# The first weight unit behind five norms takes x times the gain, and the root factor and the shift come to its result

## The chip, the cores and the metric

The kernel runs on one core of one Trainium2 chip. Its time is the device time of one execution in microseconds (us); for the kernel before there are three runs. Engines: TensorE (PE) does the matrix products, VectorE (DVE) and ScalarE (ACT) work elementwise, GpSimd (POOL) issues one stream of DMAs, SyncE (SP) another. Each engine takes its own instructions in program order, and engines wait for each other on semaphores.

## The reference

Two blocks follow one another on one sequence of 512 tokens with 1024 features. The first has six residual branches, each behind a norm whose result is scaled and shifted by a condition. Cut to what matters here:

```
rms_norm(x, g)   = x * rsqrt(mean(x*x) + eps) * g
modulate(h)      = h * (1 + scale) + shift

norm 0: x += 0.5 * gate * swiglu(h)        norm 3: x += 0.5 * gate * swiglu(h)
norm 1: x += gate * pool_mixer(h)          norm 4: x += gate * conv_mixer(h)
norm 2: x += 0.5 * gate * swiglu(h)        norm 5: x += 0.5 * gate * swiglu(h)

swiglu(h)        = (silu(h @ w_a) * (h @ w_b)) @ w_out        (1024 -> 2816 -> 1024)
conv_mixer(h)    = (b * causal_conv3(c * v)) @ w_out,  b, c, v = h @ w_in
```

After a final norm the second block takes x through norm 6, attention and a gated linear attention whose branches are merged and projected back, and then through norm 7:

```
x = x + gate2 * (square(relu(modulate(rms_norm(x, norm2)) @ w_mlp1)) @ w_mlp2)      (1024 -> 4096 -> 1024)
```

All is f32. The scale and the gain are per feature, the root factor is per token.

## The kernel before

**Layout.** Features lie on the partitions: x is `X`, eight tiles (k = 0 to 7) of 128 features by 512 tokens. A product's stationary operand is a 128x128 piece of a weight, its moving operand a 128x512 tile of the activations.

**Products.** Each f32 product is made of three in a 32-bit format that keeps fewer bits: weight high x h high (L1684), weight high x h low (L1685), weight low x h high (L1686). Weights are cut into numbered units of 128x2048 (a pair of result tiles over all eight k, 16 x 3 = 48 products; the output projections of an FFN have units of 128x1408, one result tile, 33 products). SyncE loads a unit into one of two slots of `W_RAW`; ScalarE casts it to `W_HI` (`split_hi`, L584); VectorE subtracts to get `W_LO` (`split_lo`, L979); TensorE multiplies (`products`). ScalarE casts unit u + 1 once the products of unit u - 1 are done, so weights are ready one unit ahead. An FFN is two halves of 11 input units and 8 output units. The units are numbered through the whole program: the four FFNs begin at `U_FFN`, 0, 39, 77 and 131; the pool mixer is `U_POOL`, 38; the conv mixer `U_CONV`, 115 (8 units for c and v, 4 for b, 4 for the output); `U_WO`, 204, is the merge's projection (4 units) and `U_MLP`, 208, the MLP in four quarters of 8 units.

**Results.** A unit's two result tiles lie in two PSUM banks of its slot. In an FFN ScalarE reads the first with silu (L648) and VectorE multiplies by the second (L1151), then splits the product into `g_hi` and `g_lo`. In the conv mixer ScalarE copies c (L730). In the MLP ScalarE reads with relu (L963). An output unit's result is added to x by VectorE (`add_branch`, L1136).

**A norm.** ScalarE squares each tile of x (`squares`, L592), VectorE adds the squares up in `SSQ` (`square_sums`, L1046), all but the last. TensorE sums over the partitions by 4 + 4 one-column products (`norm`, L1696 for the sum, L1700 for the last square), ScalarE takes the root (`root`, behind a table load, L594), VectorE the reciprocal and a diagonal matrix of it (`rstd_diag`, L1097, L1101), and a product with a matrix of ones spreads the factor over all partitions into bank 5 (`norm_rows`, L1706). Then for each tile VectorE multiplies x by the gain and by the factor (`normed`, L1108), ScalarE adds the shift and rounds to `h_hi` (L630), and VectorE makes `h_lo` (L1115). `GAIN` is (1 + scale) times the norm's gain, `MODS` holds the shift. The next unit's products take h tile by tile. Behind an FFN the squares of tiles 0 to 4 begin in its last output unit but one (`EARLY`); what the last tile needs comes after its addition. Behind the conv and merge projections six sums are made in the last unit; behind the pool mixer all squares and sums come after the additions to x.

**Order.** Every engine's list is written out by hand, in the order of the code; nothing is scheduled. `each(engine, count, pre, post, step)` unrolls `pre` steps, loops over pairs and unrolls `post` steps. Semaphores count: `evac_done` units taken out of PSUM, `pe_done` units multiplied, `hi_done` and `lo_done` units split, `sq_made`, `sq_summed`, `ms_made`, `rt_made`, `rs_made`, `diag_made`, `rb_made` the steps of the norm, `xr_made`, `h_hi_made`, `h_ready` those of h.

## Time and profile before

| | |
|---|---|
| median of 3 runs | 2879.02 us (2878.36 to 2879.14) |
| the profiled execution's own time | 2876.3 us |
| its span | 2874.6 us |
| TensorE busy | 2775.0 us, 97% of the span |
| VectorE busy | 1513.7 us, 53% |
| ScalarE busy | 834.3 us, 29% |
| chain that ended last | PE 91%, DVE 5%, ACT 2%, DMA 1%, issue 1% |
| mean granted TensorE clock | 0.983 of full speed |
| DMA | 353.41 MB, mean 123 GB/s |

The span is the time from the first to the last record of one execution; the execution's own time is 1.7 us above it. Busy time counts an engine's work without its waits. The chain is followed back from the last instruction, at each step to what released it. A timeline row gives the start in us from the span's start, how long, the engine, the line of the code, the result and its operands; in brackets stands how long the engine had been idle and whose work released it. Matmuls overlap: a row of 0.39 is a product's own duration, and the next starts before its end.

### The profile page before, as it was taken

Reading aid. Unit: us, or ns where it says so; the run is one execution under the profiler, and the core shown is the slowest. Engines: PE = TensorE matmul, PEld = TensorE weight load, DVE = VectorE, ACT = ScalarE, POOL = GpSimd, SP = SyncE. Lnnn points to the kernel's source line nnn. Section 1 sums busy time; section 2 is a strip of 40 time slices with the busy share of each in tenths; the row PEclk is TensorE's granted clock in tenths of the full one; section 3 lists DMA queues with packets and bytes.
Section 4 is the critical chain, followed back from the end, with each engine's and each line's share of the span. In section 5 each row is a group of like instructions: output and inputs, shape, how many; then the busy total and the mean of one; then the engine's idle time right before and its main releaser. Section 6 shows DMA issues by size and latency. Waiting matters only on the chain.

```text
span 2874.6 us, 33649 instructions
## 1 busy us (share of the span) xinstructions
PE 2775.0 (97%) x13142; PEld 2317.9 (81%) x13142; DVE 1513.7 (53%) x2032; ACT 834.3 (29%) x913; POOL 75.6 (3%) x151
## 2 busy tenths in 40 slices
PE   6999998999999999999999999999999999899999
PEld 5888877888878888788788887888898878778887
DVE  6635545636457366544663445656666533454343
ACT  3212233212132121322322333444545422222211
POOL 0100000000000000000000000000000000000000
PEclk9999998999999999999999999999999999999999
DMA  7734522635436355222363422111111342222322
GB/s 274 244 128 170 187 89 95 227 109 197 151 112 229 116 189 178 93 91 99 123 215 109 139 95 94 45 38 55 56 35 41 118 146 91 84 88 88 102 92 84
DMA packets 92932, 353.41 MB, mean 123 GB/s; under 512 B 10529, under 2 KB 11297, under 8 KB 84001
## 3 DMA queue, kind: packets, MB, share of 16 engines
q1 hardware_dynamic: 73120, 250.05, 26.0%
q0 software_dynamic: 19280, 101.23, 9.8%
q8 instruction: 70, 1.15, 0.2%
q10 hardware_dynamic: 432, 0.75, 0.1%
q14 instruction: 30, 0.24, 0.0%
HBM read 343.60 MB, written 8.39 MB: 122 GB/s over the span
## 4 chain that ended last, share of the span: by engine, by line
PE 91%; DVE 5%; ACT 2%; DMA 1%; issue 1%; SPq 0%; DVEq 0%; ACTq 0%
PE ps L1684 24%; PE ps L1685 24%; PE ps L1686 24%; PE ps L1832 4%; PE ps L1834 4%; PE ps L1833 4%; PE ps L2074 1%; PE ps L2068 1%; DMA w_raw<-in_units 1%; PE ps L2022 1%; DVE w_raw_lo L979 1%; DVE h_lo L1115 1%; PE ps L1927 0%; PE ps L1706 0%; PE ps L1992 0%
## 5 line engine op out<-in xcount | busy, mean ns | idle before, releaser
L1684 PE MATMUL ps<-h_hi,w_hi 128*128 128x512 f32 x2016 | 791.7, 393 | 21.5 <-DVE h_lo L1115 17.8
L1685 PE MATMUL ps<-h_lo,w_hi 128*128 128x512 f32 x2016 | 789.8, 392 | 0.0
L1686 PE MATMUL ps<-h_hi,w_lo 128*128 128x512 f32 x2016 | 789.2, 391 | 0.0
L584 ACT CAST w_hi<-w_raw 128x2048 fp32r<-128x2048 f32 (+1 forms) x240 | 422.1, 1759 | 633.5 <-PE ps L1686 535.8
L979 DVE TENSOR_TENSOR w_lo<-w_raw,w_hi 128x2048 fp32r<-128x2048 f32 (+1 forms) x219 | 458.4, 2093 | 129.4 <-ACT w_hi L584 129.2
L1684 PEld LDWEIGHTS ps<-h_hi,w_hi 128*128 128x128 f32 x2016 | 382.1, 190 | 112.2 <-issue 29.1
L1686 PEld LDWEIGHTS ps<-h_hi,w_lo 128*128 128x128 f32 x2016 | 381.7, 189 | 80.0
L1685 PEld LDWEIGHTS ps<-h_lo,w_hi 128*128 128x128 f32 x2016 | 381.9, 189 | 78.9
L1684 PE MATMUL ps<-g_hi,w_hi 128*128 128x512 f32 x960 | 373.6, 389 | 0.0
L1685 PE MATMUL ps<-g_lo,w_hi 128*128 128x512 f32 x960 | 373.5, 389 | 0.0
L1686 PE MATMUL ps<-g_hi,w_lo 128*128 128x512 f32 x960 | 373.5, 389 | 0.0
L1136 DVE SCALAR_TENSOR_TENSOR x_res<-ps,gate,x_res 128x512 f32<-128x512 f32 (+1 forms) x120 | 87.5, 749 | 388.9 <-PE ps L1686 380.2
L648 ACT ACTIVATE silu_a<-ps 128x512 f32<-128x512 f32 x88 | 52.7, 599 | 680.4 <-PE ps L1686 680.3
L1151 DVE TENSOR_TENSOR g_t<-silu_a,ps 128x512 f32<-128x512 f32 x88 | 60.5, 687 | 338.0 <-ACT silu_a L648 338.0
L984 DVE SCALAR_TENSOR_TENSOR ada<-ada,cond 128x1024 f32<-128x1024 f32 x176 | 208.1, 1219 | 5.5 <-DMA ada<-in_ada_t 5.4
L1684 PEld LDWEIGHTS ps<-g_hi,w_hi 128*128 128x128 f32 x960 | 180.2, 188 | 37.4
L1686 PEld LDWEIGHTS ps<-g_hi,w_lo 128*128 128x128 f32 x960 | 180.2, 188 | 37.3
L1685 PEld LDWEIGHTS ps<-g_lo,w_hi 128*128 128x128 f32 x960 | 180.2, 188 | 37.3
L1832 PE MATMUL ps<-h_hi,w_hi 128*128 128x512 f32 (+3 forms) x304 | 121.9, 401 | 3.5 <-DVE h_lo L1115 3.4
L1834 PE MATMUL ps<-h_hi,w_raw_lo 128*128 128x512 f32 (+3 forms) x304 | 114.3, 376 | 0.0
L1833 PE MATMUL ps<-h_lo,w_hi 128*128 128x512 f32 (+3 forms) x304 | 114.0, 375 | 0.0
L1832 PEld LDWEIGHTS ps<-h_hi,w_hi 128*128 128x128 f32 (+1 forms) x304 | 57.1, 188 | 21.4 <-DVE h_lo L1115 7.3
(300 smaller groups left out, 2751.0 us busy)
## 6 DMA issues: line engine op xcount, KB each, us to landing
w_raw<-in_units SPq DMA_DIRECT2D x350, 512.0 KB, 4.5
ada<-in_ada_t POOLq DMA_DIRECT2D x56, 1024.0 KB, 6.8
w_raw<-in_units SPq DMA_DIRECT2D x128, 352.0 KB, 3.7
ada<-in_ada_t POOLq DMA_DIRECT2D x64, 512.0 KB, 5.0
ada_first<-in_ada_t SPq DMA_DIRECT2D x8, 1024.0 KB, 17.7
x_res<-in_x SPq DMA_DIRECT2D x4, 512.0 KB, 7.8
x_home<-x_res POOLq DMA_DIRECT2D x1, 2048.0 KB, 6.6
attn_home<-attn_out POOLq DMA_DIRECT2D x8, 256.0 KB, 2.3
```

The costliest lines, as they stand in the source:

```text
L584: nc.scalar.copy(W_HI[u.slot][:, 0:n], W_RAW[u.slot][:, 0:n]).then_inc(hi_done, 1)
L648: nc.scalar.activation(SA[u.slot][:], BANK[2 * u.slot][:], ACT.Silu).then_inc(silu_made, 1)
L979: nc.vector.tensor_tensor(w_lo(u)[:, 0:n], W_RAW[u.slot][:, 0:n], W_HI[u.slot][:, 0:n].bitcast(F32), ALU.subtract).then_inc(lo_done, 1)
L984: return nc.vector.scalar_tensor_tensor(tile, tile, 1.0, COND[cond][:], ALU.mult, ALU.mult, accum_out=MOD_SUMS[:, bass.ds(n.v, 1)])
L1136: return nc.vector.scalar_tensor_tensor(x, bank[:], GATE[:, bass.ds((m + 8 * gate).v, 1)], x, ALU.mult, ALU.add)
L1151: nc.vector.tensor_tensor(GT[u.slot][:], SA[u.slot][:], BANK[2 * u.slot + 1][:], ALU.mult).then_inc(evac_done, 1)
L1684: pe.matmul(dst, hi[:, k, c], rhs_hi(k), start=(k == 0), stop=False)
L1685: pe.matmul(dst, hi[:, k, c], rhs_lo(k), start=False, stop=False)
L1686: last = pe.matmul(dst, lo[:, k, c], rhs_hi(k), start=False, stop=(k == kt - 1))
L1832: pe.matmul(dst, a_hi, b_hi, start=first, stop=False)
L1833: pe.matmul(dst, a_hi, b_lo, start=False, stop=False)
L1834: return pe.matmul(dst, a_lo, b_hi, start=False, stop=last)
```

## The change

At the norms 2, 3, 4, 5 and 7 the first unit's products no longer take h. They take x times the gain, split into high (`raw_hi`, ScalarE) and low part (`raw_lo`, VectorE) as soon as each tile of x is final; it lies where h will lie, and at norm 7 where the attention's operand lay. With u the weights, the result is completed by

h @ u = factor * ((x * gain) @ u) + shift @ u,

where `shift_sums` (VectorE) multiplies each of the unit's eight 128x256 weight parts by its column of the shift and adds them up in `SW`, and two one-column products with ones turn that into two columns of bank 7. `raw_out` (VectorE) copies them, and multiplies the two result tiles by the factor, which ScalarE has copied from bank 5 to `SSQ`; `raw_gated`, and the bias of ScalarE's silu, copy or relu, add the columns. TensorE's sums over the squares go inside that unit (`raw_first`), after k = 3 (norms 2, 5, 7) or k = 1 (norms 3, 4), the spreading product after k = 4 or k = 2. The second unit takes h as before; its two weight splits stand before the h split on ScalarE and ahead of it on VectorE, and the third unit's splits behind k = 5 on ScalarE and at the head of `raw_out` on VectorE. At norms 3 and 4 the squares begin one output unit earlier; the output units after the loop are four instead of two; at norm 2 sums and low parts stand between the additions to x of the pool mixer; the first quarter of the MLP stands outside its loop. Some semaphores are merged (`const_landed`, `cv_tap`, `in_landed[3]`, `a_hi_made`) to make room for five new ones.

Its core:

```diff
-        EARLY = {OUT_UNITS - 2: range(5), OUT_UNITS - 1: (5, 6)}
+        EARLY = {r: {OUT_UNITS - 3: range(5), OUT_UNITS - 2: (5,), OUT_UNITS - 1: (6,)} if r in (3, 4) else
+                 {OUT_UNITS - 3: (), OUT_UNITS - 2: range(5), OUT_UNITS - 1: (5, 6)} for r in FFN_NEXT}
...
+        RAW = [2, 3, 4, 5, 7]
+        RAW_UNIT = {2: U_FFN[1], 3: U_FFN[2], 4: U_CONV, 5: U_FFN[3], 7: U_MLP}
+        UX_HI = {r: A_HI if r == 7 else H_HI for r in RAW}
+        UX_LO = {r: A_LO if r == 7 else H_LO for r in RAW}
...
+            def raw_hi(r, k):
+                act.wait_ge(mod_done, r + 1)
+                nc.scalar.activation(UX_HI[r][:, k, 0:T], X[:, k, :], ACT.Identity, scale=GAIN[:, 8 * r + k:8 * r + k + 1]).then_inc(ux_hi_made, 1)
...
+                    if r in RAW and (r not in (5, 7) or k >= 4):
+                        raw_hi(r, k)
...
             def h_hi(r, g, ahead=None):
 
+                if r in RAW:
+                    split_hi(at(ahead))
                 for k in range(KD):
                     act.wait_ge(xr_made, KD * r + k + 1)
+                    if r in RAW:
+                        act.wait_ge(ux_used, KD * RAW.index(r) + k + 1)
                     nc.scalar.activation(H_HI[:, k, 0:T], NT[k % 4][:], ACT.Identity,
                                          bias=MODS[:, 24 * g + k:24 * g + k + 1]).then_inc(h_hi_made, 1)
-                    if ahead is not None and k == 3:
+                    if ahead is not None and r not in RAW and k == 3:
                         split_hi(at(ahead))
+                    if r in RAW and k == 5:
+                        split_hi(at(ahead + 1))
+                if r in RAW:
+                    act.wait_ge(rb_made, r + 1)
+                    nc.scalar.copy(SSQ[:], BANK[5]).then_inc(us_made, 1)
...
+                        if first:
+                            act.wait_ge(us_made, 3 * RAW.index(FFN_NORM[f]) + 2)
+                            nc.scalar.activation(SA[u.slot][:], GT[u.slot][:], ACT.Silu, bias=RSTD4[:, 28:29]).then_inc(silu_made, 1)
+                            return
...
+                    act.wait_ge(evac_done, U_CONV + 12 + 2)
+                    for k in range(4):
+                        raw_hi(5, k)
...
                     square_sums(r, tiles)
+                    if r in RAW:
+                        raw_lo(r, tiles)
                     rstd_diag(r)
+                    if r in RAW:
+                        split_lo(at(ahead))
...
+            def raw_lo(r, tiles):
+                for k in tiles:
+                    dve.wait_ge(ux_hi_made, KD * RAW.index(r) + k + 1)
+                    nc.vector.scalar_tensor_tensor(UX_LO[r][:, k, 0:T], X[:, k, :], GAIN[:, 8 * r + k:8 * r + k + 1],
+                                                   UX_HI[r][:, k, 0:T].bitcast(F32), ALU.mult, ALU.subtract).then_inc(ux_made, 1)
+            def shift_sums(r):
+                u, q = RAW_UNIT[r], KD * RAW.index(r)
+                w = W_RAW[u % 2]
+                dve.wait_ge(landed[u % 2], 32 * (u // 2) + 32)
+                dve.wait_ge(mod_done, r + 1)
+                for k in range(KD):
+                    part, shift = w[:, 2 * P * k:2 * P * (k + 1)], MODS[:, 24 * r + k:24 * r + k + 1]
+                    if k == 0:
+                        nc.vector.tensor_scalar(SW[:], part, shift, None, ALU.mult).then_inc(sw_made, 1)
+                    else:
+                        dve.wait_ge(sw_made, q + k)
+                        nc.vector.scalar_tensor_tensor(SW[:], part, shift, SW[:], ALU.mult, ALU.add).then_inc(sw_made, 1)
+            def raw_out(r):
+                u, q = at(RAW_UNIT[r]), 3 * RAW.index(r)
+                s = u.slot
+                split_lo(u + 2)
+                dve.wait_ge(pe_done, u.base + 1)
+                nc.vector.tensor_copy(RSTD4[:, 28:30], BANK[7][:, 0:2])
+                dve.wait_ge(us_made, q + 1)
+                nc.vector.tensor_tensor(GT[s][:], BANK[2 * s], SSQ[:], ALU.mult).then_inc(us_made, 1)
+                nc.vector.tensor_tensor(GT[1 - s][:], BANK[2 * s + 1], SSQ[:], ALU.mult).then_inc(evac_done, 1)
+                dve.wait_ge(evac_done, u.base + 1)
+            def raw_gated(r, dst, other):
+                s, q = RAW_UNIT[r] % 2, 3 * RAW.index(r)
+                nc.vector.scalar_tensor_tensor(dst, GT[1 - s][:], RSTD4[:, 29:30], other, ALU.add, ALU.mult).then_inc(us_made, 1)
+                dve.wait_ge(us_made, q + 3)
...
+                                if m.base == OUT_UNITS - 2:
+                                    shift_sums(FFN_NEXT[f])
...
+                if j.i is None and j.base == 3:
+                    shift_sums(5)
                 split_lo(u + 1)
...
+                for tiles in ((), (range(2),), (range(2, 4),), (range(4, 6), range(6, 8)))[gi]:
+                    square_sums(2, tiles)
+                    raw_lo(2, tiles)
+            norm_split(2, 2, U_FFN[1] + 1, ())
             ffn(1)
...
+            def raw_first(r):
+                u, q = at(RAW_UNIT[r]), KD * RAW.index(r)
+                s = u.slot
+                pe.wait_ge(lo_done, u.base + 1)
+                pe.wait_ge(evac_done, u.base - 1)
+                hi = W_HI[s][:].rearrange("p (k m) -> p k m", k=KD)
+                lo = W_LO[s][:].rearrange("p (k m) -> p k m", k=KD)
+                for k in range(KD):
+                    pe.wait_ge(ux_made, q + k + 1)
+                    for m in range(2):
+                        dst, c = BANK[2 * s + m], slice(m * P, (m + 1) * P)
+                        pe.matmul(dst, hi[:, k, c], UX_HI[r][:, k, 0:T], start=(k == 0), stop=False)
+                        pe.matmul(dst, hi[:, k, c], UX_LO[r][:, k, 0:T], start=False, stop=False)
+                        last = pe.matmul(dst, lo[:, k, c], UX_HI[r][:, k, 0:T], start=False, stop=(k == KD - 1))
+                    last.then_inc(ux_used, 1)
+                    if k == (3 if r in (2, 5, 7) else 1):
+                        norm_sums(r)
+                    if k == (4 if r in (2, 5, 7) else 2):
+                        norm_rows(r)
+                pe.wait_ge(sw_made, q + KD)
+                for m in range(2):
+                    last = pe.matmul(BANK[7][:, m:m + 1], SW[:, m * P:(m + 1) * P], ONES[:, 0:1], start=True, stop=True)
+                last.then_inc(pe_done, 1)
```

In `order`'s rows below a line number, the operation, result and operands (buffer names with their numbers) and in brackets the semaphores that are waited for are given; x5 means five alike in a row. The first place is VectorE's list around the last two output units of the third FFN, at norm 4 (`ssq` is the sum of squares, `shift_w` is `SW`; in the list after, the low part of x times the gain has the name `h_lo`, since it lies there). Before:

```order
L979 TENSOR_TENSOR w_lo<-w_raw,w_hi 128x1408 [waits hi_done]
L1042 TENSOR_TENSOR ssq<-g_t_70,g_t_71 128x512 [waits sq_made]
L1046 TENSOR_TENSOR ssq<-ssq,g_t_70 128x512 [waits sq_summed,sq_made]
L1046 TENSOR_TENSOR ssq<-ssq,g_t_71 128x512 [waits sq_summed,sq_made]
L1046 TENSOR_TENSOR ssq<-ssq,g_t_70 128x512 [waits sq_summed,sq_made]
L1136 SCALAR_TENSOR_TENSOR x_res<-ps,gate,x_res 128x512 [waits pe_done]
L979 TENSOR_TENSOR w_lo<-w_raw,w_hi 128x2048 [waits hi_done]
L1046 TENSOR_TENSOR ssq<-ssq,g_t_71 128x512 [waits sq_summed,sq_made]
L1046 TENSOR_TENSOR ssq<-ssq,g_t_70 128x512 [waits sq_summed,sq_made]
L1136 SCALAR_TENSOR_TENSOR x_res<-ps,gate,x_res 128x512 [waits pe_done]
L1097 RECIPROCAL rstd<-rstd 128x4 [waits rt_made]
L1101 TENSOR_TENSOR diag<-ident,rstd 128x512 [waits rs_made]
```

After:

```order
L1201 SCALAR_TENSOR_TENSOR h_lo<-x_res,gain,h_hi 128x512 [waits ux_hi_made] x5
L1240 SCALAR_TENSOR_TENSOR x_res<-ps,gate,x_res 128x512 [waits pe_done]
L1040 TENSOR_TENSOR w_lo<-w_raw,w_hi 128x1408 [waits hi_done]
L1107 TENSOR_TENSOR ssq<-ssq,g_t_71 128x512 [waits sq_summed,sq_made]
L1201 SCALAR_TENSOR_TENSOR h_lo<-x_res,gain,h_hi 128x512 [waits ux_hi_made]
L1213 TENSOR_SCALAR shift_w<-w_raw,mods 128x256 [waits mod_done,w_landed1]
L1216 SCALAR_TENSOR_TENSOR shift_w<-w_raw,mods,shift_w 128x256 [waits sw_made] x7
L1240 SCALAR_TENSOR_TENSOR x_res<-ps,gate,x_res 128x512 [waits pe_done]
L1040 TENSOR_TENSOR w_lo<-w_raw,w_hi 128x2048 [waits hi_done]
L1107 TENSOR_TENSOR ssq<-ssq,g_t_70 128x512 [waits sq_summed,sq_made]
L1201 SCALAR_TENSOR_TENSOR h_lo<-x_res,gain,h_hi 128x512 [waits ux_hi_made]
L1240 SCALAR_TENSOR_TENSOR x_res<-ps,gate,x_res 128x512 [waits pe_done]
```

The low parts of x and the eight operations on the weights with the shift now stand between the sums, ahead of the weight split (L1040) that the next unit's products wait for; the reciprocal and the diagonal (L1097, L1101 before) have moved behind these rows.

The second place is TensorE's list at the same norm. Before:

```order
L1686 MATMUL ps<-g_hi,w_lo 128x512
L1696 MATMUL ps<-ones_d,ssq 128x1 [waits sq_summed]
L1696 MATMUL ps<-ones_d,ssq 128x1 x3
L1700 MATMUL ps<-ones_d,g_t_71 128x1 [waits sq_made]
L1700 MATMUL ps<-ones_d,g_t_71 128x1 x3
L1706 MATMUL ps<-diag,ones 128x512 [waits diag_made]
L1684 MATMUL ps<-h_hi,w_hi 128x512 [waits h_ready,evac_done,lo_done]
L1685 MATMUL ps<-h_lo,w_hi 128x512
L1686 MATMUL ps<-h_hi,w_lo 128x512
```

After:

```order
L1854 MATMUL ps<-h_hi,w_lo 128x512
L1877 MATMUL ps<-ones_d,ssq 128x1 [waits sq_summed]
L1877 MATMUL ps<-ones_d,ssq 128x1 x3
L1881 MATMUL ps<-ones_d,g_t_71 128x1 [waits sq_made]
L1881 MATMUL ps<-ones_d,g_t_71 128x1 x3
L1852 MATMUL ps<-h_hi,w_hi 128x512 [waits ux_made]
L1853 MATMUL ps<-h_lo,w_hi 128x512
L1854 MATMUL ps<-h_hi,w_lo 128x512
L1852 MATMUL ps<-h_hi,w_hi 128x512
L1853 MATMUL ps<-h_lo,w_hi 128x512
L1854 MATMUL ps<-h_hi,w_lo 128x512
L1886 MATMUL ps<-diag,ones 128x512 [waits diag_made]
```

Before, the unit's products follow the spreading product with `diag`. After, the first row is the last product of k = 1 (`h_hi` is here x times the gain): the eight sum products stand behind k = 1, the spreading product behind the six of k = 2.

The third place is VectorE's list behind norm 5, from the last of h to the third unit. Before:

```order
L979 TENSOR_TENSOR w_lo<-w_raw,w_hi 128x2048 [waits hi_done]
L1108 SCALAR_TENSOR_TENSOR silu_a_68<-x_res,gain,ps 128x512 [waits h_ready]
L1115 SCALAR_TENSOR_TENSOR h_lo<-g_t_71,mods,h_hi 128x512 [waits h_hi_made]
L1108 SCALAR_TENSOR_TENSOR silu_a_69<-x_res,gain,ps 128x512 [waits h_ready]
L1115 SCALAR_TENSOR_TENSOR h_lo<-silu_a_68,mods,h_hi 128x512 [waits h_hi_made]
L1115 SCALAR_TENSOR_TENSOR h_lo<-silu_a_69,mods,h_hi 128x512 [waits h_hi_made]
L1151 TENSOR_TENSOR g_t_71<-silu_a_69,ps 128x512 [waits silu_made]
L1154 CAST g_hi<-g_t_71 128x512 [waits evac_done]
L1156 TENSOR_TENSOR g_lo<-g_t_71,g_hi 128x512 [waits g_hi_made]
L979 TENSOR_TENSOR w_lo<-w_raw,w_hi 128x2048 [waits hi_done]
L1151 TENSOR_TENSOR g_t_70<-silu_a_68,ps 128x512 [waits silu_made]
L1154 CAST g_hi<-g_t_70 128x512 [waits evac_done]
```

After:

```order
L1176 SCALAR_TENSOR_TENSOR h_lo<-silu_a_68,mods,h_hi 128x512 [waits h_hi_made]
L1176 SCALAR_TENSOR_TENSOR h_lo<-silu_a_69,mods,h_hi 128x512 [waits h_hi_made]
L1040 TENSOR_TENSOR w_lo<-w_raw,w_hi 128x2048 [waits hi_done]
L1224 COPY rstd<-ps 128x2 [waits pe_done]
L1226 TENSOR_TENSOR g_t_71<-ps,ssq 128x512 [waits us_made]
L1227 TENSOR_TENSOR g_t_70<-ps,ssq 128x512
L1233 SCALAR_TENSOR_TENSOR g_t_71<-g_t_70,rstd,silu_a_69 128x512 [waits silu_made,evac_done]
L1265 CAST g_hi<-g_t_71 128x512 [waits evac_done,us_made]
L1267 TENSOR_TENSOR g_lo<-g_t_71,g_hi 128x512 [waits g_hi_made]
L1262 TENSOR_TENSOR g_t_70<-silu_a_68,ps 128x512 [waits silu_made]
L1265 CAST g_hi<-g_t_70 128x512 [waits evac_done]
L1267 TENSOR_TENSOR g_lo<-g_t_70,g_hi 128x512 [waits g_hi_made]
```

The second unit's weight split (L979 before) has left the h split; the third unit's (L1040) stands where the products into `g_t` of the first unit begin. The first unit's result is read by a copy of two columns and two products with the factor, ahead of what was one product (L1151 before).

## Rows read from the trace of the kernel before

**Rows 1.** TensorE's waits in the whole run: total us, times, longest.
```profile
PE ps L1706 <- DVE diag L1101: 21.3, 7, 12.8
PE ps L1684 <- DVE h_lo L1115: 17.8, 9, 3.8
```

**Rows 2.** Timeline, all engines, fourth boundary: start, us, engine, line; [idle <-releaser].
```profile
1186.96 0.39 PE L1686 MATMUL ps<-g_hi,w_lo 128*128 128x512 f32 x1
...
1187.19 0.95 PE L1696 MATMUL ps<-ones_d,ssq 128*128 128x1 f32 x8
...
1188.17 0.63 ACT L592 ACTIVATE g_t<-x_res 128x512 f32<-128x512 f32 x1 [5.25 <-DVE x_res L1136]
1188.82 1.28 ACT L594 ACT_TABLE_LOAD   x1
...
1188.85 1.05 PE L1700 MATMUL ps<-ones_d,g_t 128*128 128x1 f32 x8 [0.72 <-ACT g_t L592]
1190.11 0.20 ACT L594 ACTIVATE rstd<-eps_c 128x1 f32<-128x1 f32 x1
...
1191.46 1.16 PE L1706 MATMUL ps<-diag,ones 128*128 128x512 f32 x2 [1.55 <-DVE diag L1101]
...
1195.16 0.77 PE L1684 MATMUL ps<-h_hi,w_hi 128*128 128x512 f32 x1 [2.54 <-DVE h_lo L1115]
```

**Rows 3.** Windows of that boundary's first unit: length, busy per engine, granted clock.
```profile
1195.16:1199.00 3.84, 3.83 (x9) 3.07 (x10) 3.84 (x7) 2.69 (x3) 0.00 (x0) 0.50 0.00 0
1199.30:1203.00 3.70, 3.70 (x18) 3.02 (x17) 3.13 (x3) 1.48 (x3) 0.00 (x0) 1.00 0.00 0
```

**Rows 4.** Timeline, TensorE: the last product before each of the other four.
```profile
438.27 0.29 PE L1783 MATMUL ps<-pool_tab,pool_z 128*128 128x16 f32 x2
...
816.32 0.39 PE L1686 MATMUL ps<-g_hi,w_lo 128*128 128x512 f32 x1
...
1371.79 0.39 PE L1686 MATMUL ps<-z_hi,w_lo 128*128 128x512 f32 x1
...
2507.26 0.39 PE L1686 MATMUL ps<-h_hi,w_lo 128*128 128x512 f32 x1
```

**Rows 5.** Timeline, ScalarE: first reader of each second unit's result.
```profile
479.47 0.60 ACT L648 ACTIVATE silu_a<-ps 128x512 f32<-128x512 f32 x1 [8.48 <-PE ps L1686]
...
850.11 0.60 ACT L648 ACTIVATE silu_a<-ps 128x512 f32<-128x512 f32 x1 [8.48 <-PE ps L1686]
...
1219.89 0.59 ACT L730 COPY conv_c<-ps 128x512 f32<-128x512 f32 x1 [8.48 <-PE ps L1686]
...
1407.73 0.60 ACT L648 ACTIVATE silu_a<-ps 128x512 f32<-128x512 f32 x1 [8.48 <-PE ps L1686]
...
2543.76 1.09 ACT L963 ACTIVATE silu_a<-ps 128x512 f32<-128x512 f32 x2 [8.00 <-PE ps L1686]
```

**Rows 6.** Groups by shape: line, engine, operation xcount | busy, mean ns.
```profile
L979 DVE TENSOR_TENSOR w_lo<-w_raw,w_hi 128x2048 fp32r<-128x2048 f32 x155 | 354.5, 2287 | 103.3 <-ACT w_hi L584 103.1 <-DVE conv_out L1226 0.2
L584 ACT CAST w_hi<-w_raw 128x2048 fp32r<-128x2048 f32 x175 | 333.9, 1908 | 359.5 <-PE ps L1686 261.8 <-PE ps L1834 57.8 <-DMA w_raw<-in_units 39.7
...
L979 DVE TENSOR_TENSOR w_lo<-w_raw,w_hi 128x1408 fp32r<-128x1408 f32 x64 | 103.9, 1623 | 26.1 <-ACT w_hi L584 26.1
...
L1115 DVE SCALAR_TENSOR_TENSOR h_lo<-g_t,mods,h_hi 128x512 fp32r<-128x512 f32 x32 | 23.9, 747 | 6.3 <-ACT h_hi L630 5.4
...
L630 ACT ACTIVATE h_hi<-g_t,mods 128x512 fp32r<-128x512 f32 x28 | 19.2, 718 | 24.3 <-DVE g_t L1108 24.3
```

**Rows 7.** Timeline, VectorE: three dependent operations, the first after another's result.
```profile
1210.36 0.48 DVE L1222 TENSOR_SCALAR conv_out<-conv_u,vecs 128x512 f32<-128x512 f32 x1
1210.88 0.75 DVE L1224 SCALAR_TENSOR_TENSOR conv_out<-conv_u,vecs,conv_out 128x512 f32<-128x512 f32 x1
1211.66 0.75 DVE L1226 SCALAR_TENSOR_TENSOR conv_out<-conv_u,vecs,conv_out 128x512 f32<-128x512 f32 x1
```

**Rows 8.** Timeline, ScalarE: its last work before the pool norm's squares.
```profile
432.40 1.07 ACT L698 COPY pool_z<-ps 128x512 f32<-128x512 f32 x2 [4.93 <-PE ps L1783]
```

197 lines of the change are left out of this document (138 added, 59 removed).

## The prediction

> **What bounds the kernel now.** I read the page's summary first: TensorE is busy for 2775.0 of 2874.6 us and holds 91% of the chain that ended last, so only time in which TensorE stands still, works slowly or does extra work can move the end. The second view is the list of who waited for whom on TensorE. Two entries lead it: the matmul that spreads the root factor over the partitions, waiting for VectorE's diagonal (21.3 us, of which 12.8 is one wait at the program's start), and the next unit's products waiting for the low part of h (17.8) [rows 1]. Both belong to the norms between blocks. I call five of them boundaries: pool to FFN (norm 2), FFN to FFN (3), FFN to conv (4), conv to FFN (5), merge to MLP (7). The third view is the timeline of one, norm 4 [rows 2]: the last product of the block starts at 1186.96, the next unit's first at 1195.16. Between them the last square, a table load, the column sums, the root, the diagonal and its matmul follow one another, then normed x and its two parts. The fourth is the windows: those first products run at clock 0.50, the lower level (1.2 GHz), because TensorE has stood idle; at 1199.3 it is at 1.00 (2.4 GHz) [rows 3].
>
> So the cost of a boundary is read from the last product before it to the moment at which ScalarE can read the second unit of the next block: 41.20, 33.79, 32.93, 35.94 and 36.50 us [rows 2, 4, 5], together 180.36. Two units are 96 products of 0.227 (0.23 from 1186.96 to 1187.19 in rows 2), 21.76 us. The rest is what the change can reach.
>
> **TensorE after the change.** The first unit takes x times the gain, which needs no root, so its products start when the last tile of x is nearly there, and the sums and the spreading matmul move inside it. What TensorE must still do at a boundary: one pitch 0.23, sums 0.95 + 1.05, spreading 1.16 [rows 2], two units 21.76, and two new one-column matmuls with the shift. A column call is two of the eight records of the 0.95 row, so two calls are 0.47. The reader starts 0.20 after the next product could (0.39 long, 0.23 pitch, 0.04 to be seen). Sum 25.82 us. Five: 129.1.
>
> **What stands in front of it.** Costs of the new work, none of which the trace has as such. Scaled cast on ScalarE: bounded by the square 0.63 [rows 2] and the cast with bias 0.72 [rows 6]; I take 0.72, the same operation with the column as scale. Back to back it repeats every 0.61, a square every 0.52. Low part on VectorE: 0.75, as for h [rows 6], 0.66 apart. Shift chain: one TENSOR_SCALAR and seven dependent operations over 256 columns. From below half of 0.48 and half of 0.75, from above 0.78 each, the distance of the dependent ones at 512 columns [rows 7]; I take 0.54 (0.50 long), since a fixed part remains, so 4.1 us, between 3.0 and 6.2.
>
> FFN to FFN and FFN to conv (t = 0 where the last output unit's products end; an output unit has 33 products, 7.48). The squares begin one unit earlier, at about t = -20.9, and each tile takes ScalarE 0.52 + 0.61; five tiles and two short waits for sums bring the fourth sum to -14.8. VectorE is then in one queue: low parts 5 x 0.66, x 0.75, weights' low part 1.62, sum and low part 0.73 + 0.66, shift 4.1, x 0.75, weights 2.29 [rows 6]. That is 14.1 and ends at -0.6. TensorE wants this weight part at 0: no wait, with 0.6 of cover. Then sum, low part, x to +1.4; square and cast on ScalarE to +2.7. TensorE does k = 0 and 1 (2.72), then the sums to +4.7; the table load has ended at +4.1. Root, reciprocal, diagonal: +5.9. k = 2 ends at +6.0, so the spreading matmul doesn't wait. Nothing is added: 25.8 each.
>
> Conv to FFN and merge to MLP. Shift chain and weights stand between x tiles 5 and 6. With t = 0 at the last unit's end VectorE has x 4 and 5 done at -9.3, the shift at -5.2, the weights at -3.0, five sums in turn with ScalarE's squares and casts at +1.7, two low parts at +3.1, x 6 and 7 at +4.5. The square of tile 7 is done at +5.6. TensorE does four k (5.44) before the sums, then a fifth while the root is made: 0 to 0.2 of wait. But the third unit now waits: its products need the first unit taken out of PSUM, which VectorE does only after the second unit's h. From the root's end that is a cast 1.91, weights 2.25, sixteen operations 10.6, 0.9 lost to ScalarE's next cast, weights 2.20, a copy 0.25, two products with the factor 1.3: 19.4 us. TensorE from the same moment: 0.95, 1.16, three k 4.08, 0.47, 10.88, 0.2, that is 17.7. Wait 1.6. (At the FFN boundaries five k follow, 20.3: no wait.) So 25.8 + 0.2 + 1.6: 27.5 and 27.7.
>
> Pool to FFN. ScalarE starts on squares at 433.4 [rows 8]; VectorE from 435.2 has seven sums up to tile 6's, six low parts and four x additions in turn, 11.1, until 446.3. TensorE has four k by 443.9 and waits 2.4 for the sums. Plus 0.2 and 1.6: 30.0.
>
> After: 30.0 + 25.8 + 25.8 + 27.5 + 27.7 = 136.8. Saved 180.4 - 136.8 = 43.6 us.
>
> **Edits at no cost.** Two more unrolled output units and a first MLP quarter outside the loop change rows on queues that wait for TensorE anyway. Merged semaphores wait for transfers long landed. SyncE's list is the same; the third unit's weights can load once the first unit's split is done, some 17 us before their cast. The pool norm's shift chain stands before the weights' low part and the first two x additions; the pooled products that wait for these are two groups on, released with ScalarE's copies of 432.40 [rows 8]. Price 0 to 4.1; I take 0, as VectorE has no other work there. At every other boundary (norms 0, 1, 6) nothing changes.
>
> **A rule against it.** The table load before the root takes 1.28, and the next activation starts 1.29 after it (at 1188.82 and 1190.11 in [rows 2]). The Trainium skill says otherwise (ScalarE: Activation LUTs, section What ACT_TABLE_LOAD costs): with a drain each switch to another set costs about 2.66 us. By that figure the root would come some 0.8 later at norms 3 and 4 and 1.4 at norm 7, and the result would be about 3 us worse; this trace disagrees, and I go by the row.
>
> **Sum.** The profiled execution took 2876.3 (span 2874.6); less 43.6 is 2832.7. The median of the runs shown is 2879.02, 2.7 above the profiled one: 2835.4, and I say 2836, as small gaps at each wait are more likely than none.
>
> **Rivals.**
> A. The clock still falls. There remain idle stretches (2.4 at the pool, 1.6 thrice) and two of light work. For: in norm 4 TensorE was still fast at 1191.46 after 0.7 + 1.55 idle and only slow after 2.54 more [rows 2, 3]; in the others it fell sooner. Against: no stretch now is as long. Price: nine products in 3.84 where 2.04 would do, 1.8 a boundary, 9 in all: 2845. Chance 0.13.
> B. VectorE bounds the FFN boundaries: the chain costs 6.2, not 4.1. The cover of 0.6 is gone, 1.5 at norms 3 and 4, and some 1.0 at 5 and 7: 5 us, 2841. For: no row has 256 columns from SBUF. Chance 0.12.
> C. Everything is hidden, the 2.4 and 1.6 too, because operations overlap more tightly: 7.8 less, 2828. Chance 0.06.
> D. The gain isn't there: the first units start early, but something in VectorE's queue (the weights' transfer behind which the shift chain stands) holds x back by about 8 us at each boundary: no difference, 2879. Against: the transfer is issued a unit before. Chance 0.02.
> E. Slower: TensorE stays at the lower level through both units, 0.2 more for each of 96 products, 19.2 a boundary, 96 - 43.6 = 52 worse: 2931. It decides once the level lasts over some 50 products at each boundary (8.7 saved + 1.8 already paid, over 0.2). Against: it was back after nine [rows 3]. Chance 0.01.
> The forecast, 2832 to 2840, has 0.66.
>
> About 0.2% (5.8 us) is what a measurement of this kernel can tell from no change. A, B, C and the forecast are all far beyond it: faster 0.97, same 0.02, slower 0.01. The range leaves out D and E and the outer ends of A and C: 2828 to 2848.
>
> **What would show it.** The spreading matmul's wait for the diagonal falls from 21.3 by some 7 to about 14.5, nearly all of it at the start and at norm 1, and the next products' wait for the low part of h nearly vanishes. At norms 3 and 4 the first unit follows the last output unit with no gap and clock 1.00; a wait on w_lo there means B. At norms 2, 5 and 7 the third unit's first product waits 1 to 2 us for VectorE's product into g_t. At the pool the sums wait 2 to 3 us. Clock 0.50 anywhere in a first unit means A. I'm wrong if the five intervals add up to under 130 or over 147 us.

## The result

| | before | changed |
|---|---|---|
| median, four runs each | 2879.08 us (2878.36 to 2880.78) | 2834.70 us (2832.64 to 2835.03) |
| the profiled execution's own time | 2876.3 us | 2835.03 us |
| its span | 2874.6 us | 2833.4 us |
| mean granted clock | 0.983 | 0.991 |

The ratio is 0.9846, with a 95% interval of 0.9835 to 0.9858: 1.5% faster, 44.4 us between the medians. The forecast was 2836.

The waits of TensorE changed as follows (total, times, longest), against [rows 1]:

```profile
PE ps L1886 <- DVE diag L1162: 14.6, 3, 12.8
...
PE ps L1832 <- DVE h_lo L1176: 4.3, 2, 3.8
...
PE ps L1832 <- DVE g_t L1227: 2.3, 2, 1.2
...
PE ps L1877 <- DVE ssq L1107: 1.8, 1, 1.8
```

The spreading product's wait fell from 21.3 to 14.6, of which 12.8 is the one at the program's start. The wait for the low part of h fell from 17.8 to 4.3, and 3.8 of that is a single wait, as long as the longest of before. Two entries are new: a wait for `g_t` (2.3, twice) and one for the sum (1.8, once).

Norm 4 on TensorE's timeline, which answers to [rows 2]:

```profile
1168.45 0.39 PE L1834 MATMUL ps<-g_hi,w_lo 128*128 128x512 f32 x1
...
1168.68 0.39 PE L1852 MATMUL ps<-h_hi,w_hi 128*128 128x512 f32 x1
...
1171.40 0.95 PE L1877 MATMUL ps<-ones_d,ssq 128*128 128x1 f32 x8
...
1172.21 1.03 PE L1881 MATMUL ps<-ones_d,g_t 128*128 128x1 f32 x8
...
1174.58 1.08 PE L1886 MATMUL ps<-diag,ones 128*128 128x512 f32 x2
...
1182.30 0.50 PE L1862 MATMUL ps<-ones,shift_w 128*128 128x1 f32 x4
...
1182.66 0.49 PE L1832 MATMUL ps<-h_hi,w_hi 128*128 128x512 f32 x1
```

The first unit starts 0.23 us behind the last product, one ordinary pitch. No row has a bracket: sums (1171.40, 1172.21), spreading product (1174.58) and the columns with the shift (1182.30) all stand between products, and nothing waits. Before, 8.2 us passed from the last product to the first of the next unit.

**The five intervals.** I measure from the last product before a boundary to ScalarE's read of the *third* unit, because at two norms the third unit is what now waits. Third readers before:

```profile
490.43 0.60 ACT L648 ACTIVATE silu_a<-ps 128x512 f32<-128x512 f32 x1 [8.56 <-PE ps L1686]
...
861.07 0.60 ACT L648 ACTIVATE silu_a<-ps 128x512 f32<-128x512 f32 x1 [8.56 <-PE ps L1686]
...
1230.85 0.59 ACT L730 COPY conv_c<-ps 128x512 f32<-128x512 f32 x1 [8.56 <-PE ps L1686]
...
1418.68 0.60 ACT L648 ACTIVATE silu_a<-ps 128x512 f32<-128x512 f32 x1 [8.56 <-PE ps L1686]
...
2554.64 1.09 ACT L963 ACTIVATE silu_a<-ps 128x512 f32<-128x512 f32 x2 [7.99 <-PE ps L1686]
```

Last products, and third readers, after the change (norm 4's last product is above):

```profile
438.59 0.29 PE L1966 MATMUL ps<-pool_tab,pool_z 128*128 128x16 f32 x2
...
806.14 0.39 PE L1834 MATMUL ps<-g_hi,w_lo 128*128 128x512 f32 x1
...
1345.78 0.39 PE L1834 MATMUL ps<-z_hi,w_lo 128*128 128x512 f32 x1
...
2474.61 0.39 PE L1834 MATMUL ps<-h_hi,w_lo 128*128 128x512 f32 x1
```

```profile
480.25 0.60 ACT L680 ACTIVATE silu_a<-ps 128x512 f32<-128x512 f32 x1 [8.56 <-PE ps L1834]
...
842.56 0.60 ACT L680 ACTIVATE silu_a<-ps 128x512 f32<-128x512 f32 x1 [8.56 <-PE ps L1834]
...
1204.84 0.59 ACT L768 COPY conv_c<-ps 128x512 f32<-128x512 f32 x1 [8.51 <-PE ps L1834]
...
1384.38 0.60 ACT L680 ACTIVATE silu_a<-ps 128x512 f32<-128x512 f32 x1 [7.84 <-PE ps L1834]
...
2513.41 1.09 ACT L1023 ACTIVATE silu_a<-ps 128x512 f32<-128x512 f32 x2 [4.89 <-PE ps L1834]
```

Subtraction (the last products of before are in [rows 2, 4]), and the forecast with one unit's pitch added (10.96, at norm 7 10.88: from the second readers in [rows 5] to the third ones here):

| norm | before | forecast after | after | saved |
|---|---|---|---|---|
| 2, pool to FFN | 52.16 | 41.0 | 41.66 | 10.50 |
| 3, FFN to FFN | 44.75 | 36.8 | 36.42 | 8.33 |
| 4, FFN to conv | 43.89 | 36.8 | 36.39 | 7.50 |
| 5, conv to FFN | 46.89 | 38.5 | 38.60 | 8.29 |
| 7, merge to MLP | 47.38 | 38.6 | 38.80 | 8.58 |
| sum | 235.07 | 191.5 | 191.87 | 43.20 |

The spans differ by 41.2, not 43.2. So 2.0 us were lost outside the boundaries; the part on the twelve traces below says what that is.

**Norm 2, where the clock fell.** Windows of the changed kernel from the first unit on: length, busy time of each engine with its count, granted clock, DMA share, GB/s.

```profile
438.70:446.20 7.50, 5.74 (x27) 4.44 (x25) 7.29 (x13) 4.85 (x9) 0.00 (x0) 1.00 0.00 0
446.20:452.00 5.80, 5.76 (x24) 4.67 (x25) 3.52 (x5) 2.05 (x2) 0.00 (x0) 0.63 0.01 3
452.00:458.50 6.50, 6.50 (x26) 4.99 (x25) 6.20 (x9) 2.83 (x4) 0.00 (x0) 0.81 0.48 163
```

The clock is at its upper level (2.4 GHz) while TensorE works and then waits in the first window; behind that wait and the one-column sums it is granted at the lower level (1.2 GHz) for part of the next two, and it is back at 1.00 from 458.50 on. From the sums at 446.24 to the second unit's first product (458.06) took 11.82 us; the same instructions at norm 5 took 8.72 (1351.73 to 1360.45): 3.1 us lost by TensorE. The interval did not grow by all of it: in a second trace of the same kernel (run 9 below), where the lower clock lasted for less time, it is 40.27 and not 41.66, and there VectorE's work sets it. So the clock cost 1.4 net, and took the place of the wait that the forecast had for the third unit. The wait itself:

```profile
446.24 1.05 PE L1877 MATMUL ps<-ones_d,ssq 128*128 128x1 f32 x8 [1.79 <-DVE ssq L1107]
```

and VectorE's queue ahead of it, with the start of each of its rows there:

```profile
441.46 1.40 DVE L1240 SCALAR_TENSOR_TENSOR x_res<-ps,gate,x_res 128x512 f32<-128x512 f32 x2
...
442.78 1.48 DVE L1107 TENSOR_TENSOR ssq<-ssq,g_t 128x512 f32<-128x512 f32 x2
...
444.17 1.41 DVE L1201 SCALAR_TENSOR_TENSOR h_lo<-x_res,gain,h_hi 128x512 fp32r<-128x512 f32 x2
...
445.50 0.68 DVE L1107 TENSOR_TENSOR ssq<-ssq,g_t 128x512 f32<-128x512 f32 x1
```

VectorE adds tiles 6 and 7 to x (441.46), makes two sums and two low parts, and only then the last sum (445.50). It is never idle there: the sum is late because it stands behind other work.

### The profile page after: what moved, and what is told of

Read it like the earlier page. It is cut to its first block, busy times and chain, and to the rows that moved or that the text cites. A ratio compares the mean times of both kernels' runs of the same rounds, so it can differ in the third digit from the quotient of the medians.

```text
span 2833.4 us, 33678 instructions
## 1 busy us (share of the span) xinstructions
PE 2763.5 (98%) x13162; PEld 2310.5 (82%) x13162; DVE 1563.2 (55%) x2127; ACT 861.6 (30%) x958; POOL 75.6 (3%) x151
## 4 chain that ended last, share of the span: by engine, by line
PE 90%; DVE 5%; ACT 2%; DMA 1%; issue 1%; SPq 0%; DVEq 0%; ACTq 0%
PE ps L1832 23%; PE ps L1833 23%; PE ps L1834 23%; PE ps L2017 4%; PE ps L2018 4%; PE ps L2019 4%; PE ps L2259 1%; PE ps L2253 1%; DMA w_raw<-in_units 1%; PE ps L2207 1%; DVE w_raw_lo L1040 1%; DVE h_lo L1176 1%; DVE w_lo L1040 0%; PE ps L2112 0%; ACT w_hi L592 0%
## 5 line engine op out<-in xcount | busy, mean ns | idle before, releaser
L1832 PE MATMUL ps<-h_hi,w_hi 128*128 128x512 f32 x1936 | 756.7, 391 | 10.4 <-DVE h_lo L1176 4.3
L1833 PE MATMUL ps<-h_lo,w_hi 128*128 128x512 f32 x1936 | 755.1, 390 | 0.0
L1834 PE MATMUL ps<-h_hi,w_lo 128*128 128x512 f32 x1936 | 755.0, 390 | 0.0
L1040 DVE TENSOR_TENSOR w_lo<-w_raw,w_hi 128x2048 fp32r<-128x2048 f32 (+1 forms) x219 | 458.3, 2093 | 133.0 <-ACT w_hi L592 132.8
L1832 PEld LDWEIGHTS ps<-h_hi,w_hi 128*128 128x128 f32 x1936 | 364.7, 188 | 90.0 <-issue 11.0
L1834 PEld LDWEIGHTS ps<-h_hi,w_lo 128*128 128x128 f32 x1936 | 364.5, 188 | 76.2
L1833 PEld LDWEIGHTS ps<-h_lo,w_hi 128*128 128x128 f32 x1936 | 364.7, 188 | 75.1
L1240 DVE SCALAR_TENSOR_TENSOR x_res<-ps,gate,x_res 128x512 f32<-128x512 f32 x120 | 87.5, 748 | 354.1 <-PE ps L1834 349.7
L2017 PE MATMUL ps<-w_hi,h_hi 128*128 128x256 f32 x240 | 70.0, 292 | 4.0 <-DVE w_raw_lo L1040 4.0
```

Of the source, the lines that this page charges most:

```text
L1040: nc.vector.tensor_tensor(w_lo(u)[:, 0:n], W_RAW[u.slot][:, 0:n], W_HI[u.slot][:, 0:n].bitcast(F32), ALU.subtract).then_inc(lo_done, 1)
L1240: return nc.vector.scalar_tensor_tensor(x, bank[:], GATE[:, bass.ds((m + 8 * gate).v, 1)], x, ALU.mult, ALU.add)
L1832: pe.matmul(dst, hi[:, k, c], rhs_hi(k), start=(k == 0), stop=False)
L1833: pe.matmul(dst, hi[:, k, c], rhs_lo(k), start=False, stop=False)
L1834: last = pe.matmul(dst, lo[:, k, c], rhs_hi(k), start=False, stop=(k == kt - 1))
L2017: pe.matmul(dst, a_hi, b_hi, start=first, stop=False)
```

## The experiments

Ten runs: nine other kernels, and the changed kernel once more (9). An expectation's "theory A" is the account of the prediction. All intervals are measured as in the table above; times are medians, and "before" beside them is the kernel before on the same chip in the same rounds. The changed kernel itself ran again only as 9 (2832.99, beside 2834.70 in its first runs), so where one of 1 to 8 is set against it, differences of under 2 us between medians say nothing and the intervals decide.

**1. The root ahead of the products again**

```diff
+                norm_sums(r)
+                norm_rows(r)
                 for k in range(KD):
                     pe.wait_ge(ux_made, q + k + 1)
...
-                    if k == (3 if r in (2, 5, 7) else 1):
-                        norm_sums(r)
-                    if k == (4 if r in (2, 5, 7) else 2):
-                        norm_rows(r)
```

> The changed kernel, but at all five boundaries TensorE's column sums and the spreading product stand ahead of the first unit's products again; everything else of the change stays. Measured from the last product before a boundary to ScalarE's first read of the third unit, the five intervals are 52.16, 44.75, 43.89, 46.89, 47.38 us before the change (235.1) and 41.66, 36.42, 36.39, 38.60, 38.80 behind it (191.9). Theory A (the gain is that products run while the root is made): the products wait for the diagonal again, and at norms 2, 5 and 7 also for sums that now stand behind the low parts. Norms 3 and 4: before less 3.1 (from the spreading product to the first product) less 0.4 plus 0.5 for the columns, 41.0. Norms 5 and 7: that plus 3.0 of later sums, about 47. Norm 2: 49.7. Together 226, so 34 us above the changed kernel, about 2869. Theory B (the gain is that h's own chain leaves the path, and the order on VectorE; the place of the root doesn't matter): at most 1.5 a boundary, under 2843.

Measured: 2870.3 us (10 runs, 2868.2 to 2872.57) beside 2877.92; ratio 0.9974 (0.9964 to 0.9983). Intervals 48.59, 41.91, 42.27, 47.48, 47.96: 228.21. Two of its waits, at norm 4 and at norm 5:

```profile
1186.30 2.08 PE L1884 MATMUL ps<-diag,ones 128*128 128x512 f32 x2 [2.16 <-DVE diag L1162]
...
1370.43 1.84 PE L1875 MATMUL ps<-ones_d,ssq 128*128 128x1 f32 x8 [5.65 <-DVE ssq L1107]
```

With the order turned back, the wait for the diagonal is there again (2.16), and at norm 5 the sum is now waited for 5.65 us, nearly twice the 2.9 of the kernel before, because VectorE makes low parts and the shift chain first. Of the 43.2 us, 36.3 (228.21 - 191.87) hang on the one thing that products run while the root is made. The price holds with the rest of the change in place: 2.8 and 2.6 of it, at norms 5 and 7, are waits for the sum beyond those of the kernel before (5.65 and 5.49 instead of 2.89), since VectorE's order is made for the new place of the sums. The 36.3 contains slow products as well as idle time: the mean granted clock is back at 0.983, that of the kernel before, from 0.991. How it divides between the two isn't measured here. Theory B is refuted. The other 6.9 are left with the root in front: 3.6 at norm 2, 2.8 and 1.6 at norms 3 and 4, and a loss of 0.6 each at 5 and 7.

**2. The earlier sums alone, without the new first unit**

```diff
--- before.py
...
-        EARLY = {OUT_UNITS - 2: range(5), OUT_UNITS - 1: (5, 6)}
+        EARLY = {r: {OUT_UNITS - 3: range(5), OUT_UNITS - 2: (5,), OUT_UNITS - 1: (6,)} if r in (3, 4) else
+                 {OUT_UNITS - 3: (), OUT_UNITS - 2: range(5), OUT_UNITS - 1: (5, 6)} for r in FFN_NEXT}
...
+                for tiles in ((), (range(2),), (range(2, 4),), (range(4, 6), range(6, 8)))[gi]:
+                    square_sums(2, tiles)
-            norm_split(2, 2, U_FFN[1] + 1)
+            norm_split(2, 2, U_FFN[1] + 1, ())
```

> The kernel before, with two parts of the change alone: at norms 3 and 4 the squares and sums begin one output unit earlier, and at the pool norm the squares' sums stand between the additions to x. No unit takes x times the gain. Theory A: at norms 3 and 4 the last square waits for the last tile of x alone, so nothing changes (44.7 and 43.9). At the pool norm TensorE's wait of 6.73 us for the sum shrinks, since VectorE has four idle us before the last group's end: 52.16 to about 48. Together some 4 us faster than before, about 2875. Theory B (early sums carry a good part of the change's gain): 5 us or more at each of norms 3 and 4 too, under 2866.

Measured: 2875.97 us (10 runs) beside 2877.92; ratio 0.9994 (0.9984 to 1.0003), so not told from no change by its time. Intervals 49.19, 44.80, 44.75, 48.42, 47.36. At norm 2:

```profile
442.16 1.87 PE L1699 MATMUL ps<-ones_d,ssq 128*128 128x1 f32 x8 [3.70 <-DVE ssq L1047]
```

The wait for the sum fell from 6.73 in the trace before to 3.70, and the interval by 3.0, where theory A had 4. At norm 3 it moved by 0.05; at norm 4 it grew by 0.9, and at norm 5, where no code changed, by 1.5. The same instructions were slower there: the spreading product of norm 4 took 2.08 instead of the 1.16 in [rows 2], the sums of norm 5 1.87 instead of 1.05; the granted clock was 0.50 from 1188.00 to 1192.00 and from 1374.00 to 1378.00. Theory B (5 us or more at norms 3 and 4) is refuted: the last square waits for the last tile of x, whatever is done earlier.

**3. The shift chain twice**

```diff
-                for k in range(KD):
+                for n in range(2 * KD):
+                    k = n % KD
                     part, shift = w[:, 2 * P * k:2 * P * (k + 1)], MODS[:, 24 * r + k:24 * r + k + 1]
+                    if n:
+                        dve.wait_ge(sw_made, q + n)
```

> The changed kernel with the shift chain computed twice at each boundary (eight more operations, 3.97 us by the trace), the second time with the same result. Theory A (VectorE's queue is what the sums and the first weights hang on, with 1.17 us of cover at norms 3 and 4 and 0.05 at norms 5 and 7): intervals longer by 2.8 at norms 3 and 4, by 3.9 at 5 and 7, and by 0 to 3 at the pool norm, where VectorE is idle for 4.2 us behind the chain. Together 13.4 to 16.4, and up to 2 more a boundary where the idle time lets the clock fall: 2848 to 2860. Theory B (the chain lies in idle time of VectorE): under 3 us in all.

Measured: 2850.71 us (2 runs); intervals 40.13, 39.53, 39.48, 45.12, 43.76. TensorE's waits at norm 3 and norm 5:

```profile
808.20 0.50 PE L1854 MATMUL ps<-h_hi,w_hi 128*128 128x512 f32 x1 [2.77 <-DVE w_lo L1040]
...
1360.71 1.87 PE L1879 MATMUL ps<-ones_d,ssq 128*128 128x1 f32 x8 [2.90 <-DVE ssq L1107]
```

At norms 3 and 4 TensorE waits 2.77 for the weights' low part: 3.97 more work less the 1.17 of cover is 2.80. Both intervals grew by 3.1. At norm 5 the wait is in two places, 0.76 for the weights (at 1352.03) and 2.90 for the sum, 3.7 together. The interval grew by 6.5: the third unit's 1.1 went, and the other 3.9 came with the clock, which was at 0.50 from 1360.70 to 1367.00 and at 0.73 for the six us behind; at norm 7 it grew by 5.0, with 0.58 and 0.88 in such windows. At norm 2 nothing was added (40.13, beside 41.66 and 40.27 in the two traces of the changed kernel): the chain lies in time in which VectorE was idle. So the forecast's free shift chain at norm 2 holds, and elsewhere the chain is as near to the path as said.

**4. The sums later at norms 3 and 4**

```diff
-                    if k == (3 if r in (2, 5, 7) else 1):
+                    if k == 3:
                         norm_sums(r)
-                    if k == (4 if r in (2, 5, 7) else 2):
+                    if k == 4:
                         norm_rows(r)
```

> The changed kernel with the sums after k = 3 and the spreading product after k = 4 at norms 3 and 4 too. Theory A (the third unit waits where less than 19.1 us of TensorE's work lies between the spreading product and it; two k fewer are 2.7, and the slack there is 1.1 to 1.6): the third unit waits 1.1 to 1.6 at norms 3 and 4, as it does for 1.12 and 1.17 at 5 and 7; intervals 37.5 to 38.0 instead of 36.4, in all 2 to 3 us slower, 2837.5. Theory B (the wait at 5 and 7 comes from what is special there): intervals stay at 36.4.

Measured: 2836.60 us (2 runs); intervals 38.21 and 38.22 at norms 3 and 4, 0.2 above theory A's upper end, the others as in the changed kernel. Norm 3:

```profile
831.66 0.50 PE L1832 MATMUL ps<-h_hi,w_hi 128*128 128x512 f32 x1 [1.08 <-DVE g_t L1227]
```

The wait of 1.08 (1.14 at norm 4) is that of norms 5 and 7. It lengthens the interval by more than its idle time: the product before starts at 830.20, 1.46 earlier, where the pitch is 0.23; small gaps at the last tile of h and behind the wait make up the rest of the 1.8. It is the distance between the spreading product and the third unit that decides, not what is special at norms 5 and 7.

**5. The sums later at norm 2**

```diff
-                    if k == (3 if r in (2, 5, 7) else 1):
+                    if k == {2: 4, 3: 1, 4: 1, 5: 3, 7: 3}[r]:
                         norm_sums(r)
-                    if k == (4 if r in (2, 5, 7) else 2):
+                    if k == {2: 5, 3: 2, 4: 2, 5: 4, 7: 4}[r]:
                         norm_rows(r)
```

> The changed kernel with the pool norm's sums after k = 4 instead of 3 and its spreading product after k = 5. There TensorE stood idle for 1.79 us before the sums, and then ran 17 products and the sums at the lower clock (window 446.2 to 452.0: 0.63), some 3.1 us lost. Theory A (the idle time brought the clock down; with products of k = 4 in it the engine waits only 0.6 for their low part): no lower clock, interval 36.4 + 0.6 and a wait of the third unit of 2 to 2.6 instead of none, 39.3 against 41.66: 2 us faster, 2832.5. Theory B (the clock falls at this place anyway, after the pool mixer's small products): the interval stays or grows by up to 1.3.

Measured: 2833.24 us (2 runs); norm 2's interval 40.39, against 41.66 (2.4 less was expected). The same stretch as above:

```profile
446.00:452.00 6.00, 6.00 (x34) 4.78 (x33) 3.93 (x7) 2.67 (x4) 0.00 (x0) 1.00 0.01 3
452.00:458.00 6.00, 4.71 (x23) 3.91 (x23) 5.87 (x8) 2.59 (x4) 0.00 (x0) 1.00 0.50 175
```

The clock stays at 1.00, so theory A's first half holds: with 0.53 us of idle time, ahead of the six products before the sums, in place of 1.79 right before them it didn't fall. But the second unit now waits 1.29 for h and the third 1.11 for `g_t`. Time gained at the clock went into waits, and against the 40.27 of the changed kernel's second trace nothing was gained.

**6 and 7. Norms 5 and 7: the sums after k = 1, then the shift chain earlier too**

Kernel 6 has the first two changes, kernel 7 all of them (and the same at norm 7):

```diff
-                    if k == (3 if r in (2, 5, 7) else 1):
+                    if k == (3 if r == 2 else 1):
-                    if k == (4 if r in (2, 5, 7) else 2):
+                    if k == (4 if r == 2 else 2):
...
                     raw_lo(5, range(4))
+                    shift_sums(5)
...
-                if j.i is None and j.base == 3:
-                    shift_sums(5)
```

> The changed kernel with the sums after k = 1 and the spreading product after k = 2 at norms 5 and 7 too (as at 3 and 4). Theory A (there VectorE's last sum, 5.9 us behind the last product, sets the root): TensorE waits 2.7 us for it, the root comes no earlier, the third unit no longer waits, and the interval grows by 2.7 less 1.1, so 1.6 each, with up to 2 more where the clock falls: 2838 to 2842. Theory B (the position after k = 3 is what made the third unit wait): 1.1 us less each, 2832.5.

Measured: 2841.21 us (2 runs); intervals at norms 5 and 7 42.62 and 42.47, so 4.0 and 3.7 more. The sums wait at norm 5:

```profile
1350.07 1.86 PE L1877 MATMUL ps<-ones_d,ssq 128*128 128x1 f32 x8 [2.85 <-DVE ssq L1107]
```

It is 2.85 us (2.68 at norm 7). Less the third unit's wait, which is gone, that is a loss of 1.7 and 1.3 (at norm 7 also without the 0.19 before the spreading product); the other 2.3 and 2.4 are put down to the clock, 0.50 from 1350.00 to 1356.00 and 0.56 from 2482.40 to 2488.40. Theory A by the time; the intervals lie just above its 3.6 a boundary.

> As the run with sums after k = 1 at norms 5 and 7, and there the shift chain stands one output unit earlier, in 3.94 us for which VectorE was idle. Theory A (the chain delays the last sum by its length, since VectorE is behind there): the sums are ready at about +3 us, nothing waits, and both intervals come to those of norms 3 and 4, 36.4: 2.2 and 2.4 less, 2830.2. Theory B (ScalarE's squares or the weights' split delay the sum, not the chain): a wait of 1 us or more stays before the sums.

Measured: 2834.86 us (2 runs); intervals 38.46 at norm 5 and 37.18 at norm 7. The sums wait 0.17 and 0.18 instead of 2.85 and 2.68, so the chain was what made the sum late, and no third unit waits. Theory B is refuted, but against the changed kernel norm 5 gained only 0.14 of the 2.2 expected, and norm 7 1.6 of 2.4. Windows at norm 5:

```profile
1348.80:1354.00 5.20, 5.20 (x25) 3.76 (x26) 3.37 (x5) 3.11 (x5) 0.00 (x0) 0.80 0.00 0
```

and at norm 7:

```profile
2478.30:2483.50 5.20, 5.02 (x27) 3.85 (x28) 2.98 (x5) 4.37 (x6) 0.00 (x0) 1.00 0.00 0
```

The same instructions behind the same idle time (0.17 and 0.18) ran at clock 0.80 at norm 5 (0.83 in the four us behind) and at 1.00 at norm 7.

**8. The third unit's weight split behind the products with the factor**

```diff
-                split_lo(u + 2)
                 dve.wait_ge(pe_done, u.base + 1)
...
                 nc.vector.tensor_tensor(GT[1 - s][:], BANK[2 * s + 1], SSQ[:], ALU.mult).then_inc(evac_done, 1)
+                split_lo(u + 2)
```

> The changed kernel with the third unit's weight split (2.2 us) behind the two products with the factor instead of ahead of them, at all five. Theory A (the third unit needs both, and VectorE does both after the second unit's h): its wait of 1.12 and 1.17 at norms 5 and 7 stays, now on w_lo; no difference, 2834.7. Theory B (it waits for the PSUM banks alone, the weights have time): the waits vanish, 2.3 us faster.

Measured: 2832.10 us (2 runs, 2831.14 to 2833.07); intervals 41.66, 36.39, 36.39, 38.67, 38.73, so as before the edit to 0.1. The wait is still there and has changed its name:

```profile
1372.80 0.49 PE L1832 MATMUL ps<-h_hi,w_hi 128*128 128x512 f32 x1 [1.19 <-DVE w_lo L1040]
```

The third unit needs both the banks and its weights, and VectorE makes one after the other in either order. The time is 2.6 below the changed kernel's first median without any gain at the boundaries; see the next part.

**9 and 10. The changed kernel again, and one with three places mended**

```diff
-                    if k == (3 if r in (2, 5, 7) else 1):
+                    if k == {2: 3, 5: 2, 7: 2}.get(r, 1):
                         norm_sums(r)
-                    if k == (4 if r in (2, 5, 7) else 2):
+                    if k == {2: 4, 5: 3, 7: 3}.get(r, 2):
                         norm_rows(r)
...
                     raw_lo(5, range(4))
+                    shift_sums(5)
...
-                for tiles in ((), (range(2),), (range(2, 4),), (range(4, 6), range(6, 8)))[gi]:
-                    square_sums(2, tiles)
-                    raw_lo(2, tiles)
+                if gi:
+                    square_sums(2, ((), range(2), range(2, 4), range(4, 7))[gi])
+                    raw_lo(2, ((), range(2), range(2, 4), range(4, 8))[gi])
```

(and the shift chain of norm 7 one output unit earlier likewise)

> The changed kernel once more, beside the next run on the same chip. 2834.7, and the five intervals 41.7, 36.4, 36.4, 38.6 and 38.8, while stretches outside them differ by some us from one profiled execution to the next, without a change of code: the one from norm 5's third unit to the last product before norm 7 took 1088.58 before the change and 1090.23 behind it.

> The changed kernel with three places mended. Norms 5 and 7: the shift chain one output unit earlier, the sums after k = 2 and the spreading product after k = 3. Norm 2: the last sums stand ahead of the low parts of tiles 4 to 7. Theory A: at 5 and 7 the sums are there before TensorE asks, with no idle time and so no lower clock, and the third unit has 1.36 us more of cover than its wait of 1.1 to 1.2: intervals 36.4 and 36.6. At norm 2 the sums come 1.3 us earlier, TensorE stands idle 0.6 instead of 1.8, the clock stays, and the third unit waits 1.1: 38.2. Together 184.0 against 191.9, 7.9 us less: 2827. Theory B (TensorE's clock falls in this light stretch however short the idle time is, as at norm 5 in the run before): up to 3 a boundary given back, 2830 to 2834.

Measured, five runs each beside nine of the kernel before (2877.77):

| | median | ratio to before, 95% | intervals | sum |
|---|---|---|---|---|
| changed, again | 2832.99 (2830.37 to 2834.50) | 0.9843 (0.9829 to 0.9856) | 40.27, 36.39, 36.43, 38.63, 38.81 | 190.53 |
| three places mended | 2827.83 (2825.92 to 2830.04) | 0.9828 (0.9814 to 0.9841) | 39.16, 36.39, 36.38, 36.85, 36.84 | 185.62 |

The mended kernel is the fastest of all, 5.2 us below the changed one by the medians (no run of it is above the lowest of the changed one: 2830.04 against 2830.37); the intervals to before overlap, so the traces have to say where it comes from. At norms 5 and 7 the intervals fell by 1.8 and 2.0 (1.75 and 1.96 against the first trace); 0.4 and 0.2 less than expected, as the third unit still starts 0.51 and 0.61 behind the product before it, where the pitch is 0.23. At norm 2 TensorE's wait is 0.67 instead of 1.80:

```profile
445.23 1.05 PE L1875 MATMUL ps<-ones_d,ssq 128*128 128x1 f32 x8 [0.67 <-DVE ssq L1107]
```

```profile
446.20:452.00 5.80, 5.80 (x22) 4.30 (x22) 5.11 (x7) 2.05 (x2) 0.00 (x0) 0.71 0.00 0
```

There the clock fell all the same (0.71), behind 0.67 us of idle time: this much of theory B is true. But it is not why the interval is 39.16 and not the 38.2 expected, as the next paragraph shows.

**What sets the third unit, and when the clock costs nothing.** From ScalarE's root on, VectorE has the second unit's weight split, h, the third unit's split and the two products with the factor to do. At eighteen boundaries of seven traces the third unit starts 19.33 to 19.46 us behind the start of the root: at norms 5 and 7 of both traces of the changed kernel and of kernels 4, 5, 8 and 10, at norms 3 and 4 of kernel 4, and at norm 2 of kernels 3, 5 and 10 and of run 9. That is VectorE's chain. Wherever else products run while the root is made, TensorE gets there later by itself, 19.99 us or more behind the root. A lower clock therefore costs only what it takes beyond VectorE's chain. Norm 5 shows it. Kernels 4 and 5 and run 9 have there the code of the changed kernel, and in all three the clock was at 0.50 for some 3 us. First the changed kernel's first trace, then run 9, with the root, a window and, for run 9, the third unit's start:

```profile
1353.72 0.27 ACT L639 ACTIVATE rstd<-ps,eps_c 128x4 f32<-128x4 f32 x1 [0.93 <-PE ps L1881]
```

```profile
1351.88 0.26 ACT L639 ACTIVATE rstd<-ps,eps_c 128x4 f32<-128x4 f32 x1 [0.93 <-PE ps L1881]
...
1352.90:1355.90 3.00, 3.00 (x6) 1.64 (x6) 2.11 (x2) 1.03 (x1) 0.00 (x0) 0.50 0.00 0
...
1371.24 0.50 PE L1832 MATMUL ps<-h_hi,w_hi 128*128 128x512 f32 x1
```

In the first trace the clock is 1.00 all through and the third unit starts at 1373.07, 19.35 behind the root, after a wait of 1.12. In run 9 it starts 19.36 behind the root without a wait: the slow products have filled the idle time. The intervals are 38.60 and 38.63 (38.59 and 38.58 in kernels 4 and 5). At norm 2 of kernel 10 the root is at 447.21 and the third unit starts at 466.56, 19.35 behind it: VectorE's chain again, so the fallen clock cost nothing there, and the expected 38.2 had the third unit's wait too short.

**Where the 2 us outside the boundaries went.** With the boundaries cut out, each trace leaves six stretches in which no edit touches TensorE's products. From the twelve traces (before, changed, and the ten experiments):

| stretch | shortest to longest |
|---|---|
| start to norm 2 | 436.87 to 439.17 |
| norm 2 to 3, norm 3 to 4 | 325.89 to 325.90 |
| norm 4 to 5 | 140.94 to 140.94 |
| norm 5 to 7 (attention and its neighbours) | 1086.69 to 1091.12 |
| norm 7 to the end | 319.93 to 320.01 |

Four of them repeat to 0.1 us. The first varies by 2.3, and the one with norm 6, attention and the gated linear attention by 4.4, with the same code. The profiled execution before had 438.27 and 1088.58 there, the changed one 438.59 and 1090.23: 1.97 us, which is the gap between 43.2 and 41.2. One such loss in the changed kernel's trace stands behind a wait of 3.69 for h that both traces have: its products are 0.63 long and 0.43 apart up to 2433.80, while in the trace before the same products stand 0.23 apart from the ninth on (2465.76). From the end of that wait to the last product before norm 7 it is 46.06 against 44.91, so 1.15 of the 1.65 lost in this stretch. So this is put down to the spread of single executions, and not to the change; kernel 8's lower time too (1086.69, the shortest).

## Why the prediction was right

**The mechanism, shown.** The forecast laid the gain on products that run while the root is made, with the shift and the factor applied to their result on VectorE. Kernel 1 takes that one thing back and loses 36.3 of the 43.2 us; kernel 2, which has the earlier sums alone, gains 0.6 over its boundaries (3.0 at norm 2, less 2.4 at norms 4 and 5).

**The sum.** Forecast 43.6 for the five intervals, measured 43.2; no single boundary is off by more than 0.8. Two small slips don't matter: 19.4 less 17.7 is 1.7 and not 1.6, and 25.8 + 0.2 + 1.6 is 27.6, where 27.5 and 27.7 are taken.

- *Costs of the new work*, against the estimates 0.72, 0.75 and 4.1 for the chain:

```profile
L1201 DVE SCALAR_TENSOR_TENSOR h_lo<-x_res,gain,h_hi 128x512 fp32r<-128x512 f32 x32 | 22.5, 745 | 3.0 <-ACT h_hi L597 3.0
L597 ACT ACTIVATE h_hi<-x_res,gain 128x512 fp32r<-128x512 f32 x32 | 22.4, 710 | 0.0
...
L1216 DVE SCALAR_TENSOR_TENSOR shift_w<-w_raw,mods,shift_w 128x256 f32<-128x256 f32 x35 | 17.0, 485 | 1.2
```

The scaled cast is 0.71, the low part 0.745 and one operation of the chain 0.485 (estimate 0.50 long, 0.54 apart). That is between half of the 512-column operation's 0.75 and its whole, nearer the half, as estimated. The first operation and the seven others together take 4.0.

- *Norms 3 and 4*, nothing waits: right. The cover was put at 0.6 and is 1.17 (the weights' low part ends at 805.20, TensorE asks at 806.37); kernel 3 shows by the wait of 2.77 that the cover is of this size. The intervals are 0.4 shorter than forecast.
- *Norms 5 and 7*, the third unit waits for VectorE: right in place and cause, 1.12 and 1.17 instead of 1.6. Two rows of norm 5, VectorE's and TensorE's:

```profile
1369.47 2.29 DVE L1040 TENSOR_TENSOR w_lo<-w_raw,w_hi 128x2048 fp32r<-128x2048 f32 x1
...
1372.34 0.68 DVE L1227 TENSOR_TENSOR g_t<-ps,ssq 128x512 f32<-128x512 f32 x1
```

```profile
1373.07 0.50 PE L1832 MATMUL ps<-h_hi,w_hi 128*128 128x512 f32 x1 [1.12 <-DVE g_t L1227]
```

The forecast's 19.4 for VectorE's chain from the root's end to the third unit is the best of its terms: it is 19.35 from the root's start. The split for the third unit (1369.47) stands behind the last of h, and the second product with the factor ends at 1373.02; 0.05 later TensorE starts. Kernel 4 brings the same wait to norms 3 and 4, kernels 6 and 7 take it away. In the changed kernel's second trace the wait at norm 5 isn't there, because slow products fill it, with the same interval. So it is the chain that was forecast rightly; whether a wait shows depends on the clock.

- *Norm 2*: a wait of 1.79 for 2.4, in the place that was named. But the third unit's wait of 1.6 isn't there, and rival A happened: the clock fell behind the wait, TensorE lost 3.1 by it (rival A had 1.8 a boundary), and that time filled the third unit's wait and went 1.4 beyond it. The forecast of 30.0 against 30.7 is thus partly luck: without the 1.4 it is 29.3 (the second trace, 40.27 less the pitch of 10.96), so the work was put 0.7 too high and the clock's loss at nothing.
- *The table load*: 1.28 long, and the next activation 1.29 behind its start, as in [rows 2]:

```profile
1170.93 1.28 ACT L609 ACT_TABLE_LOAD   x1
...
1172.22 0.20 ACT L609 ACTIVATE rstd<-eps_c 128x1 f32<-128x1 f32 x1
```

By the Trainium skill (ScalarE: Activation LUTs, section What ACT_TABLE_LOAD costs) a switch would cost about 2.66 with a drain. The trace after, too, has the load alone: nothing of a drain stands before it (the cast ahead ends at 1170.91) or behind it.

**Rivals.** A: at one boundary of five in the first trace, norm 2, and at two in the second, norms 2 and 5. Its price of 1.8 a boundary was 1.4 at norm 2 in the first and nothing at norm 5, since there VectorE's chain was longer; "clock 0.50 anywhere in a first unit" is a sign of it, but says nothing of the time. B: no chain of 6.2, and kernel 3 shows what such a one would have cost; 3.97 more gave 16.0 more in time. C, D and E didn't happen: in the first trace every first unit but norm 2's has clock 1.00, and two waits of 1.1 to 1.2 before third units remain.

**The time.** 2836 against 2834.70. The step from the profiled execution to the median was set at +2.7, from before alone. The changed kernel's own profiled execution (2835.03) lay 0.3 above its median, while its boundaries saved 43.2 and 1.97 went to stretches that vary. So two steps were off, by 3.0 and by 2.0, and nearly cancelled; with the 0.4 of the boundaries and the 0.6 added at the end they make the 1.3 by which the forecast missed. That it missed by so little is luck. The 43.6 for the boundaries rests on five sums, each within 0.8 of what was measured, with errors of both signs: 0.4 too long at norms 3 and 4, 0.7 too short at norm 2.

## What to carry to other kernels

Where a norm stands between two matmuls, the part of it that is per row can wait until behind the product: the next products then start on the unscaled operand, and only statistics, factor and a rank-one shift are late. What it costs is elementwise work, so look for the engine that does it. Here each thing put on VectorE's one queue ahead of the last sum (the shift chain, low parts) came back as a wait of TensorE once its cover was used up, and the place of the sums inside the unit trades an idle stretch before them against a wait two units on. Ask of each boundary which engine's chain sets its end: where it is VectorE's, TensorE's lower clock was free. For effects of some us in a long program, cut the trace at landmarks: unchanged stretches that repeat to 0.1 us show an edit of 1 us that the medians can't.

## What the runs showed of the hardware that was not expected

The clock behind short idle stretches and light work is not the same each time. At norm 2 six traces have the changed kernel's list for TensorE (the two of it, and kernels 4, 6, 7 and 8). Behind 1.79 or 1.80 us of idle time and the one-column sums the clock fell in all six; five intervals are 41.66 to 41.70 and one is 40.27. After 0.67 us (kernel 10) it also fell, to 0.71 over the next window. After 0.53 us (kernel 5) it stayed at 1.00. In kernel 7 the same instructions behind 0.17 and 0.18 us got 0.80 at norm 5 and 1.00 at norm 7.

It also fell without such a stretch. At norm 5 the changed kernel's TensorE has products up to 0.1 us before the sums. The clock stayed at 1.00 in its first trace and in kernel 8, and was at 0.50 for some 3 us around the spreading product in its second trace and in kernels 4 and 5. At norms 3, 4 and 7 it fell in neither trace of the changed kernel, and the third unit's wait of 1.1 to 1.2 brought it down nowhere. The length of a slow run varies too: behind the same wait of 3.69 before norm 7 seven products took 0.4 us or more from start to start in the kernel before, and thirteen in the changed one. What decides between these isn't settled by these runs.
